# Recurrent units with X in the opposite partition half, and products interleaved over the four array quarters

## What is computed

```python
def step(s, inp):                      # RWKV-7, per head, token by token
    r_t, w_t, k_t, v_t, kk_t, a_t = inp
    sa = jnp.einsum('bhvk,bhk->bhv', s, -kk_t)
    s = s * w_t[:, :, None, :] + sa[..., None] * (kk_t * a_t)[:, :, None, :] + v_t[..., None] * k_t[:, :, None, :]
    return s, jnp.einsum('bhvk,bhk->bhv', s, r_t)
```

## Time and profile before

| | us |
|---|---|
| median of 3 runs | 1522.41 (1518.60 to 1524.04) |
| span of the profiled execution, first to last instruction | 1516.7 |
| its TensorE busy (matmuls) | 1309.2 |
| its VectorE, ScalarE, GpSimd busy | 521.0, 338.1, 165.0 |

### The profile page before, as it was taken

How to read it: one execution, slowest core, us unless ns; L and a number is a source line. 1 busy time by engine, 2 the same in 40 slices (tenths; PEclk the granted TensorE clock), 3 DMA queues, 4 the chain that set the end, 5 groups by cost and what they waited for, 6 DMA issues and landing times.

```text
span 1516.7 us, 38874 instructions
## 1 busy us (share of the span) xinstructions
PE 1309.2 (86%) x16856; PEld 913.1 (60%) x16856; DVE 521.0 (34%) x1144; ACT 338.1 (22%) x671; POOL 165.0 (11%) x238
## 2 busy tenths in 40 slices
PE   5989999989998988899877669888999888998672
PEld 2448844468888457798444334445664678974441
DVE  1324444145556734011101053457555431111003
ACT  2223221143223131000000033433452300010001
POOL 2003310024333001000000030010000010000001
PEclk8999999999999989899999879987979899999997
DMA  9841159831001175899999882134314469999995
GB/s 397 304 154 59 59 202 314 298 151 59 25 37 58 56 288 195 308 386 395 385 398 415 358 296 89 78 121 173 111 56 167 177 250 331 399 393 399 391 426 191
DMA packets 42105, 354.68 MB, mean 234 GB/s; under 512 B 5707, under 2 KB 10651, under 8 KB 23664
## 3 DMA queue, kind: packets, MB, share of 16 engines
q1 hardware_dynamic: 21456, 302.11, 50.7%
q0 software_dynamic: 8704, 28.53, 5.6%
q10 hardware_dynamic: 11808, 22.03, 4.4%
HBM read 321.63 MB, written 31.01 MB: 233 GB/s over the span
## 4 chain that ended last, share of the span: by engine, by line
PE 65%; DMA 17%; DVE 7%; issue 7%; ACT 3%; POOL 1%; SPq 0%; ACTq 0%; POOLq 0%; DVEq 0%
PE PB L688 59%; DMA arena<-in_w_moe 7%; PE PB L691 6%; DMA ring<-in_w_moe 4%; DVE arena L2010 3%; DMA dispatched<-arena,rows_i 2%; DMA ring<-in_w_mod 2%; ACT arena L1540 1%; DMA arena<-dispatched 1%; DVE small L2023 1%; DMA expert_out<-arena 1%; POOL dispatched L631 1%; DVE arena L2017 1%; DVE x L2010 0%; DVE arena L2014 0%
## 5 line engine op out<-in xcount | busy, mean ns | idle before, releaser
L688 PE MATMUL PB<-arena 64*64 64x64 f32 (+6 forms) x9756 | 489.6, 294 | 48.6 <-DMA arena<-in_w_moe 30.0
L688 PEld LDWEIGHTS PB<-arena 64*64 64x64 f32 (+3 forms) x9756 | 399.8, 129 | 133.9 <-issue 69.7
L688 PE MATMUL PB<-ring,hT 128*128 128x512 f32 (+1 forms) x720 | 313.8, 591 | 7.2 <-DVE hT L2013 3.6
L688 PEld LDWEIGHTS PB<-ring,hT 128*128 128x128 f32 x720 | 137.1, 193 | 167.0 <-issue 162.4
L688 PE MATMUL PB<-ring,arena 128*32 128x256 f32 (+2 forms) x3456 | 195.3, 380 | 33.7 <-DMA ring<-in_w_moe 31.0
L688 PEld LDWEIGHTS PB<-ring,arena 128*32 128x32 f32 x3456 | 147.8, 110 | 73.0 <-issue 24.8
L1540 ACT ACTIVATE arena<-PB 128x256 f32<-128x256 f32 (+3 forms) x217 | 106.6, 491 | 331.1 <-PE PB L688 277.5
L691 PE MATMUL PB<-cst,arena 128*128 128x128 f32 (+2 forms) x758 | 118.6, 298 | 52.3 <-ACT arena L1540 17.9
L691 PEld LDWEIGHTS PB<-cst,arena 128*128 128x128 f32 (+2 forms) x758 | 91.1, 157 | 98.6 <-issue 57.9
L2431 DVE TENSOR_TENSOR arena<-arena,PB 128x256 f32<-128x256 f32 (+1 forms) x32 | 15.1, 471 | 300.9 <-PE PB L688 287.7
L688 PE MATMUL PB<-ring,scT 128*32 128x512 f32 x384 | 60.8, 753 | 21.6 <-DMA ring<-in_w_mod 16.0
(11 more groups left out here) (149 smaller groups left out, 928.9 us busy)
## 6 DMA issues: line engine op xcount, KB each, us to landing
arena<-in_w_moe SPq DMA_DIRECT2D x50, 2048.0 KB, 16.5
ring<-in_w_moe SPq DMA_DIRECT2D x46, 2048.0 KB, 14.5
ring<-in_w_mod SPq DMA_DIRECT2D x24, 2048.0 KB, 8.9
ring<-in_w_mix SPq DMA_DIRECT2D x22, 2048.0 KB, 8.6
dispatched<-gate ACTq DMA_DIRECT2D x1, 8320.0 KB, 50.4
arena<-dispatched POOLq DMA_DIRECT2D x20, 256.0 KB, 9.2
expert_out<-gate ACTq DMA_DIRECT2D x1, 3456.0 KB, 22.1
expert_out<-arena ACTq DMA_DIRECT2D x12, 288.0 KB, 8.7
```

Source lines behind the costliest of these rows:

```text
L688: return nc.tensor.matmul(out, lhsT, rhs, start=start, stop=stop, **k)
```

## The change

X, LJ and the level-0 blocks are kept in the partition half opposite to the one of XT and T1. So t1 (from LJ and X) and dx (into X) use the two other quarters of the array, and other products can be issued between theirs:

- `gram_low` writes to the opposite half (`far`). A new product gramF makes the grams' blocks once more in the opposite half, ScalarE copies it to GF, and GpSimd masks LJ from GF instead of G4. `first_blocks` (XT of level 0) still reads G4 and comes behind LJ of level 1.
- `gram` waits for all four TT, does `gram_low` (and gramF) first and then both q. VectorE makes X of level 0 first and then masks G4.
- `level_first` issues t1 with rh (level 1), `gla_turn` (3), `gla_att` (4, beside q 0) or the values product of `gla_read` (5) between its products. `level_second` issues dx and dxt in turn.
- TensorE waits for what these need ahead of t1 (`ready`): at level 1 for G of both q, at 3 for GLA's rows, at 4 for GT, at 5 for att. The rest of `gla_read` moves from behind level 4 to behind t1 of level 5.
- VectorE subtracts X of q 0, X of q 1, XT of q 0, XT of q 1.

```diff
+        GF = spare[:, 3072:3584].rearrange("p (b q j n) -> p b q j n", b=2, q=2, j=2)
+
+        def far(c):
+
+            return slice(64 - 64 * c, 128 - 64 * c)
...
                 w = (g, n, q)
-                bab = G4[:, 2 * q:2 * q + 2, :].rearrange("p b (j n) -> p b j n", j=2)[:, :, :, 0:64]
                 m4 = slice(4 * q, 4 * q + 4)
-                pool.wait_ge(*when("G", *w))
                 if v > 1:
                     pool.wait_ge(*when("t1", *w, v - 1))
-                elif n:
-                    pool.wait_ge(*when("ms", g, n - 1, 1))
-                mul(LJ8[:, m4, :].rearrange("p (b j) n -> p b j n", b=2), bab,
+                else:
+                    pool.wait_ge(*when("GF", g, n))
+                    if n:
+                        pool.wait_ge(*when("ms", g, n - 1, 1))
+                mul(LJ8[:, m4, :].rearrange("p (b j) n -> p b j n", b=2), GF[:, :, q, :, :],
                     bc(bc(lvl[:, 64 * v:64 * v + 64], 1, 2), 1, 2), "LJ", *w, v)
-                if v == 1:
-                    XT = XT8[:, m4, :]
-                    mul(XT.rearrange("p (b j) n -> p b j n", b=2), bab, bc(bc(lvl[:, 0:64], 1, 2), 1, 2))
-                    pool.wait_ge(sem("pool"), count["pool"])
-                    nc.gpsimd.tensor_tensor(XT, bc(C("eye"), 1, 4), XT, ALU.subtract).then_inc(*tick("pool", "XT", *w, 0))
+
+            def first_blocks(g, n, q, lvl):
+
+                w, XT = (g, n, q), XT8[:, 4 * q:4 * q + 4, :]
+                bab = G4[:, 2 * q:2 * q + 2, :].rearrange("p b (j n) -> p b j n", j=2)[:, :, :, 0:64]
+                pool.wait_ge(*when("G", *w))
+                mul(XT.rearrange("p (b j) n -> p b j n", b=2), bab, bc(bc(lvl[:, 0:64], 1, 2), 1, 2))
+                pool.wait_ge(sem("pool"), count["pool"])
+                nc.gpsimd.tensor_tensor(XT, bc(C("eye"), 1, 4), XT, ALU.subtract).then_inc(*tick("pool", "XT", *w, 0))
 
...
                     for v in range(1, 6):
                         for q in range(2):
                             level_blocks(g, n, q, v, lvl)
+                        if v == 1:
+                            for q in range(2):
+                                first_blocks(g, n, q, lvl)
...
             def gram(g, n):
 
+                for j in range(4):
+                    pe.wait_ge(*when("TT", g, n, j))
+                gram_low(g, n)
                 for q in range(2):
-                    for j in (2 * q, 2 * q + 1):
-                        pe.wait_ge(*when("TT", g, n, j))
-                    if q:
-                        gram_low(g, n)
                     first = (6, 4)[q]
...
+                    claim(b, "GF", g, n)
                 for j in range(4):
                     T = TT[:, j, :, :]
                     for b in range(2):
                         k = slice(64 * b, 64 * b + 64)
-                        ins = both(lambda c, r: mm(PB[r, 2 + b, 64 * j:64 * j + 64], T[k, 0, r], T[k, 2, r]))
+                        ins = both(lambda c, r: mm(PB[far(c), 2 + b, 64 * j:64 * j + 64], T[k, 0, r], T[k, 2, r]))
                 ins.then_inc(*tick("pe", "gramL", g, n))
+                for j in range(4):
+                    T = TT[:, j, :, :]
+                    for b in range(2):
+                        k = slice(64 * b, 64 * b + 64)
+                        ins = both(lambda c, r: mm(PB[far(c), b, 64 * j:64 * j + 64], T[k, 2, r], T[k, 0, r]))
+                ins.then_inc(*tick("pe", "gramF", g, n))
...
+            def level_first(q, beside):
+
+                for m in range(4):
+                    if beside:
+                        beside(q, m)
+                    ins = both(lambda c, r: mm(PB[r, q, 64 * m:64 * m + 64], LJ8[far(c), 4 * q + m, :], X8[far(c), 4 * q + m, :]))
+                return ins
+
+            def level_second(q, v, *w):
+
+                for m in range(4):
+                    at = 4 * q + m
+                    if v < 5:
+                        low = both(lambda c, r: mm(PB[far(c), q, 256 + 64 * m:320 + 64 * m], XT8[r, at, :], T18[r, at, :]))
+                    up = both(lambda c, r: mm(PB[r, 4 + q, 64 * m:64 * m + 64], T18[r, at, :], XT8[r, at, :]))
+                if v < 5:
+                    low.then_inc(*tick("pe", "dx", *w, q, v))
+                up.then_inc(*tick("pe", "dxt", *w, q, v))
...
+                def values_beside(q, m):
+                    if m % 2 == 0:
+                        gla_values(i, 2 * q + m // 2)
+
+                def ready(v):
+
+                    if v == 1:
                         for p in range(2):
                             pe.wait_ge(*when("G", g, n, p))
                         claim(2, "RH", g, n)
-                        for h in range(8):
-                            ins = both(lambda c, r: mm(PB[r, 2, 64 * place(h):64 * place(h) + 64], masked(h, 1, 0)[r, :],
-                                                       values(i, h)[r, :]))
-                        ins.then_inc(*tick("pe", "rh", g, n))
+                    if v == 3:
+                        pe.wait_ge(*when("gqk", g, n))
+                        claim(7, "GT", g, n)
+                    if v == 4:
+                        pe.wait_ge(*when("GT", g, n))
+                        claim(6, "gatt", g, n)
+                    if v == 5:
+                        pe.wait_ge(*when("gatt", g, n))
+                        claim(6, "gout", g, n)
+
+                beside = {1: rh_beside, 3: turn_beside, 4: att_beside, 5: values_beside}
...
-                    if q == 3:
-                        gla_turn(g, n)
                     if q == 5:
-                        gla_att(g, n)
                         gla_add(g, n, 0)
                         if not last:
                             prep(g, n + 1, 1, (2, 3))
-                    if q == 7:
+                    if q == 8:
                         gla_read(g, n, 0)
...
+                    ready(v)
                     for q in range(2):
                         pe.wait_ge(*when("X", g, n, q, v - 1))
                         pe.wait_ge(*when("LJ", g, n, q, v))
                         claim(q, "T1", g, n, q, v)
-                        product(q, 0, q, LJ8, X8).then_inc(*tick("pe", "t1", g, n, q, v))
+                        level_first(q, beside.get(v)).then_inc(*tick("pe", "t1", g, n, q, v))
...
                             claim(q, "X", g, n, q, v)
-                            product(q, 256, q, XT8, T18).then_inc(*tick("pe", "dx", g, n, q, v))
                         claim(4 + q, "XT", g, n, q, v)
-                        product(4 + q, 0, q, T18, XT8).then_inc(*tick("pe", "dxt", g, n, q, v))
+                        level_second(q, v, g, n)
...
+                act.wait_ge(*when("gramF", g, n))
+                fn(GF.rearrange("p b q j n -> p b (q j n)"), PB[:, 0:2, 0:256], ACT.Copy, "GF", g, n)
...
+                dve.wait_ge(*when("gramL", g, n))
+                for q in range(2):
+                    X = X8[:, 4 * q:4 * q + 4, :]
+                    tt(X.rearrange("p (b j) n -> p b j n", b=2),
+                       PB[:, 2:4, 128 * q:128 * q + 128].rearrange("p b (j n) -> p b j n", j=2),
+                       bc(bc(lvl_t[:, 0:64], 1, 2), 1, 2), ALU.mult, "L0", g, n, q)
+                    tt(X, bc(C("eye"), 1, 4), X, ALU.subtract, "X", g, n, q, 0)
...
-                    for q in range(2):
-                        m4 = slice(4 * q, 4 * q + 4)
-                        if v < 5:
+                    if v < 5:
+                        for q in range(2):
+                            m4 = slice(4 * q, 4 * q + 4)
                             dve.wait_ge(*when("dx", g, n, q, v))
                             tt(X8[:, m4, :], X8[:, m4, :], PB[:, q, 256:512].rearrange("p (h n) -> p h n", h=4),
                                ALU.subtract, "X", g, n, q, v)
+                    for q in range(2):
+                        m4 = slice(4 * q, 4 * q + 4)
                         dve.wait_ge(*when("dxt", g, n, q, v))
```

51 lines of the change are left out of this document (23 added, 28 removed).

## The result

The changed kernel is slower: median 1531.68 us (1526.90 to 1543.85, 11 runs) against 1520.62 (1516.44 to 1524.04, 11 runs), a ratio of 1.0095 (95% interval 1.0077 to 1.0113). The forecast had been 1514.2, with 0.11 on slower. So the profiles differ by 22.9 us where the medians differ by 11.1: what follows explains a bad execution of the changed kernel, and its sums in us are larger than what the medians lost. Lines are now L701 for every matmul, L704 transposes, L2068 VectorE, L547 GpSimd's multiplication.

A forecast was written before the change was run, and what follows sets the result against it. The prediction took the relay between engines and GpSimd's queue as the bound: 11.4 us saved in six units, less 3.2 for the clock, gave 8.2, so 1508.5 profiled and 1514.2 median; range 1499 to 1522.

The forecast's parts named there:

- What the clock takes: Clock falls at the new gap ahead of level 5 in four units: 0 to 6.4 us lost, half taken, 3.2.
- Price of a product: TensorE's matmul records: using all four array quarters halves the price of a record, 29.4 to 14.8 ns.
- rival C: Units' new product pairs do not overlap because both row halves write one bank: slower, 1534 us; chance 0.11.
- Level 1: Start of a unit, grams to dxt: first t1 1.8 us late, 0.6 pure wait; level ends 0.3 us later.
- my own sign: Stated test in a unit's first level: prediction wrong if that level loses more than 0.3 us net.
- Levels 4 and 5: Unit's late levels: e_exc delays GpSimd's LJ masks, TensorE idles over 2 us; 1.7 us saved per unit.
- A middle unit: Units followed by another in their group: each 1.7 us shorter, counted four times.
- The first unit of a group: Opening unit of each group: counted among the four units given 1.7 us saved each.
- The last unit of the first group: Unit without prep, so no e_exc in the way: 3.4 us saved.
- The range: Whole kernel: 1499 to 1522 us, meant to hold eight in ten.
- Rival A: TensorE stays the bound in the units, most of 36 us shows: 1486, or 1500 with half; chance 0.12.
- later stages take back what the units give: Stated test behind the units: prediction wrong if this happens; a saving in a unit should pass through to the end.

The follow-up runs named there:

- small_changed: The changed kernel with the modulation loads used in the units cut to 64 columns, third and fourth units affected; six units 275.5 us, one run.
- pool_order: The changed kernel with GpSimd multiplying e_exc behind its level 5 masks instead of ahead of them; 1524.06 us, ratio 1.0014 to before.
- small_loads: pool_order with the modulation loads used in the units cut to 64 columns, third and fourth units affected; six units 266.0 us, one run.
- small_before: The kernel before with the modulation loads used in the units cut to 64 columns, third and fourth units affected; six units 275.4 us, one run.
- pool_before: The kernel before with GpSimd multiplying e_exc behind its level 5 masks; 1520.21 us, ratio 0.9999 to before.
- gap_before: The kernel before with only the grams' order changed: all four TT awaited, gram_low first, then both q; 1525.81 us, ratio 1.0047 to before.
- pool_undone: pool_order with dx and dxt issued one behind the other again instead of in turn; 1517.22 us, ratio 0.9994 to before.

## Why the prediction was wrong

The sign was wrong. The step that failed is "What the clock takes" with its bounds of 0 and 6.4 us: falls grew by some 50 us at half clock, which I price below at 11 to 25 us. The sum also had no term for the standstills, and it gave the first unit of each group the saving of a middle one. Against the medians the forecast is off by 17.5 us (1531.7 for 1514.2).

- **Price of a product: right.** 14.7 ns a record in four quarters; rival C's mechanism did not happen.
- **Level 1: right in its steps, not in its sum.** From `gram_low` to t1 5.88 us (laid out: 5.75), G waited for 0.34 us (0.6), t1 q 0 to q 1 2.68 us (2.67). But the next unit's `prep`, which follows level 1, starts 11.82 us after the unit's start against 10.95, so 0.9 us late and not 0.3; by my own sign that part was wrong.
- **Levels 4 and 5: right.** GpSimd's LJ was late by way of e_exc, TensorE idle 1.92 us (laid out: 2.45).
- **A middle unit: right where nothing else acts.** Forecast 43.3 us, 43.78 in small_changed, so 1.2 us saved and not 1.7. With GpSimd's order too it is 41.4 to 41.9.
- **The first unit of a group: wrong.** I gave it the middle unit's 1.7 us. Neither kernel with small loads has a load in its third unit, a standstill of 0.6 us, or a fall behind the transposes at its start, and the changed one is 0.3 us longer (48.48, 48.21). Its first t1 comes 10.56 us after the unit's start against 8.17, so 2.4 us late where 1.8 was laid out; the other 1.4 us are lost behind it, at no single place.
- **The last unit of the first group: 3.4 us not seen.** 41.69 us in small_changed against 40.53 before. TensorE stood still there ("issue") for 1.43, 0.40, 0.80 and 0.93 us, 3.6 in all, and 3.3 us ran at half clock. The earlier trace rows could not show either.
- **The clock: wrong by count.** I counted one gap in each of four units and took half of them. At that gap the clock did fall four times in four. But the relay had made two gaps of over 1 us in each, and the 1.25 us ahead of `gram_low` I had put into the order of the work but not into the clock. The standstills made more, and some falls have no idle time of even half a us ahead of them. The page of the Trainium skill that I named ("TensorE: Matmul & The Clock Gate", "HAM oscillation — how this bites in real kernels") has the mechanism, a wait that brings the clock down; what failed was to apply it to the one longest gap alone. What a fall costs seems to depend on how full the unit is: 0.8 us in the changed kernel (small_changed, fifth unit 44.61 against fourth 43.78), 1.8 with pool_order (43.13 against small_loads' 41.37), 2.6 in the old one (small_before 47.53 against 44.98). Half-clock time grew by some 50 us, as much as 14 more falls of the length priced here (about 3.5 us); at 0.8 to 1.8 us each that is 11 to 25 us, an estimate from single executions.
- **The standstills: not foreseen.** Nothing in the rows shown of before hinted at them; its trace has the one of 0.69 us. The eight after add up to 9.7 us, and not all of that need be on the path.
- **The range: one sum wrong.** Rival A's "1500 where half of it does" should be 1522.4-18 = 1504. That changes nothing here.
- **Rival C's figure is luck.** 1534 lies near 1531.7, but its cause, pairs that don't overlap, is not what happened.

Against the forecast for the units, 273.4-8.2 = 265.2 us, the profiled 291.1 is 25.9 too long. In small_changed, with two loads gone and a third of the half-clock time, the units still take 275.5 us, as long as small_before's 275.4. So without most of the falls the changed kernel's units are level with the old ones and not 11.4 us faster: what is missing there is the first units of the groups, the first group's last unit, and the falls that stay (about 20 us at half clock). The parts overlap, since a standstill can itself bring a fall, so a split finer than this stays open. The third and fourth units of small_before and small_changed (3rd, 4th, then 3rd):

```profile
314.90:363.11 48.21, 47.51 (x1174) 41.35 (x1178) 23.55 (x43) 16.19 (x32) 16.54 (x21) 0.97 0.02 4
363.11:410.64 47.53, 45.84 (x1152) 38.69 (x1146) 22.83 (x42) 14.31 (x30) 16.58 (x21) 0.96 0.02 4
...
317.79:366.27 48.48, 42.35 (x1192) 35.38 (x1192) 23.44 (x43) 16.79 (x33) 16.40 (x21) 0.97 0.02 4
```

**Do the later stages take back what the units give?** In the changed kernel there was nothing to take, and yet they took longer. Behind the units the profiled executions of before, pool_before and gap_before took 1015.9 to 1020.0 us, the changed kernel and those built on it without moved loads 1021.7 to 1027.6, with the same program there. The clock goes with it: 145 to 169 us of that stretch at half clock against 168 to 193 (before 155, changed 170). Over the 16 kernels that were timed the stretch grows by about 0.26 us for each us at half clock, which would make 4 of the 4.5 us. pool_undone is the case in point: its units are 2.7 us shorter than before's, the stretch behind them 8.4 us longer, with 33 us more at half clock. Why the clock falls more often there is open, and each of these is one execution.

**Is it the fetch of instructions that waits at the standstills?** By the traces, yes: each of the 95 ends 1.2 to 1.7 us after a packet of instructions has landed, and the long ones follow an interval without such a packet. That is also why in pool_order TensorE started again only 2.7 us after the load had ended: the packet left at 468.32 and landed at 469.25, 1.45 us before the restart. That q8 is TensorE's queue is inferred (34096 of the changed kernel's 39276 instructions are TensorE's matmuls and weight loads), and so is why no packet came while the load ran; no run changed the fetch itself.
